# Delta rule: the triangular solve of both scan directions on four quadrants of the matmul array, with outputs, q k part, u and w in another order

## What is computed

```python
lower = jnp.where(strict, bc[..., :, None] * kk * decay, 0.0)
rhs = jnp.concatenate([vc * bc[..., None], kc * (bc * jnp.exp(gc))[..., None]], axis=-1)
sol = lax.linalg.triangular_solve(lower + jnp.eye(CHUNK), rhs, left_side=True, lower=True, unit_diagonal=True)
u, w = sol[..., :DV], sol[..., DV:]
qk = jnp.einsum("nbhid,nbhjd->nbhij", qc, kc) * decay

def step(S, xs):
    v_new = u_i - jnp.einsum("bhck,bhkv->bhcv", w_i, S)
    o = (jnp.einsum("bhck,bhkv->bhcv", q_i * jnp.exp(g_i)[..., None], S)
         + jnp.einsum("bhij,bhjv->bhiv", qk_i, v_new))
    S = S * jnp.exp(g_last)[..., None] + jnp.einsum("bhck,bhcv->bhkv", k_i * jnp.exp(g_last - g_i)[..., None], v_new)
```

## Time and profile before

| what | us |
|---|---|
| median of three runs | 2375.2 |
| lowest and highest of them | 2372.45 and 2375.28 |
| the profiled execution, its own time | 2375.22 |
| its span, first to last instruction | 2373.5 |
| setup of the DeltaNet phase to the first w, 404.70 to 435.72 | 31.02 |
| from the first to the eighth w, 435.72 to 740.77 | 305.05 |
| from there to the next phase, 740.77 to 775.50 | 34.73 |

### The profile page before, as it was taken

The page is one execution under the profiler, slowest core; times in us unless marked ns, Lnnn a source line. Parts: engine busy times, 40 slices in busy tenths (PEclk is TensorE's granted clock), DMA queues, the critical chain, the costliest instruction groups (busy, mean ns, idle before and its releaser), DMA issues. The chain is left out here.

```text
span 2373.5 us, 39379 instructions
## 1 busy us (share of the span) xinstructions
PE 2240.4 (94%) x15174; PEld 1811.4 (76%) x15174; DVE 1540.0 (65%) x1807; ACT 1193.4 (50%) x1387; POOL 419.5 (18%) x384
## 2 busy tenths in 40 slices
PE   5999999888988999999977999999999999999997
PEld 3777787777776777777866888888888888888885
DVE  5556311544544444464338988888989888898987
ACT  5232223233232333352216777777777676777675
POOL 6101201333231100000421101111111111111101
PEclk9999999999998999999978999999999999999998
DMA  8445542001001333166248999999999999999997
GB/s 295 160 142 159 162 122 66 3 20 38 20 20 33 100 101 107 63 219 194 107 169 306 356 385 393 385 384 384 383 382 380 383 394 385 382 384 381 382 383 283
DMA packets 271153, 557.51 MB, mean 235 GB/s; under 512 B 15672, under 2 KB 70045, under 8 KB 267965
## 3 DMA queue, kind: packets, MB, share of 16 engines
q1 hardware_dynamic: 261677, 530.16, 61.9%
q0 software_dynamic: 4752, 17.30, 2.7%
q10 hardware_dynamic: 4608, 8.39, 0.9%
HBM read 511.73 MB, written 44.07 MB: 234 GB/s over the span
## 5 line engine op out<-in xcount | busy, mean ns | idle before, releaser
L2605 PE MATMUL ps<-whigh,xeT 128*128 128x512 f32 x2048 | 657.1, 395 | 1.5 <-DVE xeT L2777 1.5
L2785 DVE TENSOR_TENSOR wlow<-hT,whigh 128x2048 fp32r<-128x2048 f32 x192 | 432.2, 2286 | 64.1 <-ACT whigh L2709 64.1
L2605 PEld LDWEIGHTS ps<-whigh,xeT 128*128 128x128 f32 x2048 | 385.8, 188 | 81.2 <-issue 1.9
L2605 PE MATMUL ps<-wlow,xeT 128*128 128x512 f32 x1024 | 399.6, 390 | 0.0
L2709 ACT ACTIVATE whigh<-hT 128x2048 fp32r<-128x2048 f32 x192 | 358.4, 1909 | 10.8 <-PE ps L2605 10.8
L2605 PE MATMUL ps<-whigh,hidT 128*128 128x512 f32 x1024 | 328.0, 391 | 0.0
L2785 DVE TENSOR_TENSOR wlow<-oaT,whigh 128x2048 fp32r<-128x2048 f32 x96 | 216.9, 2288 | 41.7 <-ACT whigh L2709 41.7
L2785 DVE TENSOR_TENSOR wlow<-obT,whigh 128x2048 fp32r<-128x2048 f32 x96 | 218.0, 2286 | 21.2 <-ACT whigh L2709 21.2
L2605 PEld LDWEIGHTS ps<-whigh,hidT 128*128 128x128 f32 x1024 | 192.3, 188 | 40.3
L2605 PEld LDWEIGHTS ps<-wlow,xeT 128*128 128x128 f32 x1024 | 193.2, 189 | 38.0
L2605 PE MATMUL ps<-wlow,hidT 128*128 128x512 f32 x512 | 199.6, 390 | 0.0
(11 more groups left out here) (329 smaller groups left out, 3554.2 us busy)
## 6 DMA issues: line engine op xcount, KB each, us to landing
hT<-in_w_down SPq DMA_DIRECT2D x66, 1024.0 KB, 10.4
obT<-in_w_up SPq DMA_DIRECT2D x64, 1024.0 KB, 10.6
hT<-in_w_up SPq DMA_DIRECT2D x64, 1024.0 KB, 8.4
hT<-in_w_gate SPq DMA_DIRECT2D x62, 1024.0 KB, 11.0
oaT<-in_w_down SPq DMA_DIRECT2D x62, 1024.0 KB, 8.8
oaT<-in_w_gate SPq DMA_DIRECT2D x34, 1024.0 KB, 10.4
obT<-in_w_gate SPq DMA_DIRECT2D x32, 1024.0 KB, 8.4
oaT<-in_w_ada SPq DMA_DIRECT2D x20, 1024.0 KB, 7.8
```

Of the source, the lines that this page charges most:

```text
L2605: mm = pe.matmul(out, lhs[x], rhs[y], start=start and i == 0, stop=stop and i == 2)
L2785: dve.tensor_tensor(wlow[slot][:, :], raw[(FIRST + x) % RAW_SLOTS], whigh[slot][:, :].bitcast(F32), ALU.subtract).then_inc(low_done, 1)
```

## The change

Level by level, both directions are now one group. y, inv_turn (the turn of the inverse, now also in level 0) and upd of levels 0 to 3 walk through four quadrants: the block in partition half h comes out in the half of its token pair, with the two source halves in two PSUM banks. POOL makes inv0 in one orientation. xb and inv hold both directions, and the transposes of x and of the q k part (xT, qkT) are separate tiles. Level 4 stays on two quadrants. The semaphores y_ps, y_sb, upd_ps, inv_done, invT_ps, invT_sb, w_ps and w_sb are no longer per direction.

The second gram product, make_qk and the turn of the q k part (qk_turn) move into levels 0 and 1 of the unit's own solve; rows of the next unit moves from level 0 to level 1, differences on DVE from levels 0 and 1 to 2 and 3. outputs is split: out_states after upd of level 3, out_chunks before upd of level 4. u is made ahead of w, and w and scan_kv are cut into four 64x64 quadrant matmuls. out_turn and tok_q stand before scan_ws of step 1; channels 1 and tok_v after scan_kv of step 1.

The functions on PE and its loop over units:

```diff
+def qk_turn(n):
+    pe.wait_ge(qk_done, n + 1)
+    pe.wait_ge(vb_done, 2 * n + 2)
+    for d in range(2):
+        mm = small_turns(2, d * HW, dec[:, d, :, :])
+    mm.then_inc(qkT_ps, 1)
+
+def to_slots(banks, left, right):
+
+    for t2 in range(TPG // 2):
+        for d in range(2):
+            for t in (2 * t2, 2 * t2 + 1):
+                for h in ((0, 1), (1, 0))[t % 2]:
+                    src = HALVES[h]
+                    lo = d * P + t2 * CHUNK
+                    mm = pe.matmul(ps[HALVES[t % 2], banks[h], lo:lo + CHUNK], left[src, d, t, :],
+                                   identc[src, :] if right is None else right[src, d, t, :], start=True, stop=True)
+    return mm
+
+def y(n, lv):
+    if lv == 0:
+        pe.wait_ge(xturn_sb, n + 1)
+        pe.wait_ge(qeT_sb, 2 * n + 2)
+        pe.wait_ge(inv0_done, 2 * n + 2)
     else:
+        pe.wait_ge(inv_done, n * LV + lv)
+    if lv < LV - 1:
+        mm = to_slots((0, 1), xT, inv)
...
+    mm.then_inc(y_ps, 1)
+
+def inv_turn(n, lv):
...
+    if lv < LV - 1:
+        mm = to_slots((4, 5), inv, None)
...
+def upd(n, lv):
+    pe.wait_ge(y_sb, n * LV + lv + 1)
+    pe.wait_ge(invT_sb, n * LV + lv + 1)
+    if lv < LV - 1:
+        for t2 in range(TPG // 2):
+            for d in range(2):
+                for h in range(2):
+                    for tp in ((0, 1), (1, 0))[h]:
+                        src = HALVES[tp]
+                        slot = 2 * t2 + h
+                        lo = d * P + t2 * CHUNK
+                        mm = pe.matmul(ps[HALVES[h], tp, lo:lo + CHUNK], invT[src, d, slot, :], xb[src, d, slot, :],
+                                       start=True, stop=True)
...
+def make_w(n):
+    pe.wait_ge(kbe_done, 2 * n + 2)
+    for d in range(2):
+        for t in range(TPG):
+            for turn_over in range(2):
+                for i, half in enumerate(HALVES):
+                    part = HALVES[(i + turn_over) % 2]
+                    lo = d * HW + t * CHUNK
+                    mm = pe.matmul(ps[part, 4 + i, lo:lo + CHUNK], kbe[d][half, t, part],
+                                   invT[half, d, t, :], start=True, stop=True)
+    mm.then_inc(w_ps, 1)
...
+    if i < NC1:
+        for turn_over in range(2):
+            for d in range(2):
+                t, half = place(chunks(d)[i])
+                part = HALVES[(d + turn_over) % 2]
+                mm = pe.matmul(ps[part, 6 + d, P:2 * P], kd[d][half, t, part], vnew[d][half, t, :],
+                               start=True, stop=True)
...
+def out_states(n):
+    if n + 2 < NU:
+        pe.wait_ge(diff_done, 2 * TPG * (n + 3))
...
+def out_chunks(n):
+    pe.wait_ge(vnew_done[0], (n + 1) * NC1)
+    pe.wait_ge(vnew_done[1], (n + 1) * NC1)
...
     for lv in range(LV):
+        y(n, lv)
+        inv_turn(n, lv)
+        if n >= 1 and lv == LV - 1:
+            out_chunks(n - 1)
         if n >= 1 and SPLIT + lv < NCHUNK:
             scan_ws(n - 1, SPLIT + lv)
+        if lv == 0:
+            gram(n, 1)
+        upd(n, lv)
+        if n >= 1 and SPLIT + lv < NC1:
             scan_kv(n - 1, SPLIT + lv)
+        if lv == 1:
+            qk_turn(n)
+            if more:
+                rows(n + 1)
+        if lv == 3:
+            if n >= 1:
+                out_states(n - 1)
+            if more:
+                tok_k(n + 1)
-    uw(n)
+    make_u(n)
+    make_w(n)
     scan_kv(n, 0)
     if more:
         channels(n + 1, 0)
+    if n >= 1:
+        out_turn(n - 1)
+    if more:
+        tok_q(n + 1)
     for i in range(1, SPLIT):
         scan_ws(n, i)
         if more:
             if i == 1:
                 gram(n + 1, 0)
             if i == 3:
+                x_turn(n + 1)
+        scan_kv(n, i)
+        if more:
+            if i == 1:
+                channels(n + 1, 1)
                 tok_v(n + 1)
+            if i == 3:
+                qe_turn(n + 1, 0)
+                qe_turn(n + 1, 1)
```

On ACT and DVE:

```diff
+def inverse_turned(n, lv):
+    act.wait_ge(invT_ps, n * LV + lv + 1)
...
+    if lv < LV - 1:
+        for d in range(2):
+            ins = act.activation(slots(invT, d, 0), crossed(4, 5, d), ACT.Copy)
+        ins.then_inc(invT_sb, 1)
...
+def mask_y(n, lv):
+    dve.wait_ge(y_ps, n * LV + lv + 1)
...
+    if lv < LV - 1:
+        for d in range(2):
+            ins = dve.tensor_tensor(slots(xb, d, 0), crossed(0, 1, d),
+                                    bcast(bcast(levelmask[:, d, lv + 1, :], 1, 2), 1, 2), ALU.mult)
+        ins.then_inc(y_sb, 1)
...
+def inverse(n, lv):
+    dve.wait_ge(upd_ps, n * LV + lv + 1)
+    if lv < LV - 1:
+        for d in range(2):
+            ins = dve.tensor_tensor(slots(inv, d, 1), slots(inv, d, 1), crossed(0, 1, d), ALU.subtract)
+        ins.then_inc(inv_done, 1)
```

More of the change, by code:

```diff
@@ L1221, in y @@
[L1221 to L1248, removed]
+                        pe.wait_ge(x_done[1], n + 1)
@@ new lines, in out_states @@
+                def out_states(n):
+                    if n + 2 < NU:
+                        pe.wait_ge(diff_done, 2 * TPG * (n + 3))
+                    else:
+                        pe.wait_ge(qk_done, NU)
+                    if n >= 1:
+                        pe.wait_ge(on_done, n)
+                    begun = set()
+                    for t in range(TPG):
+                        for d in range(2):
+                            for c in (2 * t, 2 * t + 1):
+                                if chunks(d)[0] != c:
+                                    half = place(c)[1]
+                                    pe.matmul(ps[half, 3, t * P:(t + 1) * P], qeT[n % 2][d][:, t, half], state[d][:, chunks(d).index(c), :],
+                                              start=c % 2 not in begun, stop=False, skip_group_check=True)
+                                    begun.add(c % 2)
@@ new lines, in out_chunks @@
+                def out_chunks(n):
+                    pe.wait_ge(vnew_done[0], (n + 1) * NC1)
+                    pe.wait_ge(vnew_done[1], (n + 1) * NC1)
+                    for t in range(TPG):
+                        for d in range(2):
+                            for half in HALVES:
+                                mm = pe.matmul(ps[half, 3, t * P:(t + 1) * P], qkT[n % 2][half, d, t, :], vnew[d][half, t, :],
+                                               start=False, stop=d == 1, skip_group_check=True)
+                    mm.then_inc(o_ps, 1)
@@ L1537, in _ @@
                 differences(0, 1)
-                for d in range(2):
-                    make_x(0, d)
-                    make_qk(0, d)
+                make_x(0, 0)
+                make_x(0, 1)
                 for n in range(NU):
@@ L1544, in _ @@
                         i = SPLIT + lv
[L1545 to L1551 removed]
+                        mask_y(n, lv)
@@ L1559, in _ @@
+                        inverse(n, lv)
                         if n >= 1 and i < NC1:
                             scan_state(n - 1, i)
[L1561 to L1564 removed]
+                        if lv == 0:
+                            make_qk(n)
+                        if lv == 2 and more:
+                            differences(n + 1, 0)
@@ L1583, in _ @@
+                        if i < 3 and more:
+                            make_x(n + 1, i - 1)
                 for i in range(SPLIT, NCHUNK):
```

352 lines of the change are left out of this document (155 added, 197 removed).

## The result

| | before | after |
|---|---|---|
| median of four runs | 2375.24 us (2372.45 to 2377.86) | 2340.61 us (2339.39 to 2344.19) |
| profiled execution, span | 2375.22, 2373.5 us | 2339.39, 2337.7 us |
| eighth unit's w (before) or u (after) less the first's | 305.05 us | 271.87 us |

The next phase begins at 739.65 us instead of 775.55, 35.9 earlier, and takes from there as long as before (1598.05 and 1597.95 us): all of it is in the changed phase.

The account below looks back on a forecast made before the run. PE was taken to set the pace in the DeltaNet phase: 2375.2 - 27 (shorter units) + 13 (clock falls before y) + 7 (falls in level 3) = 2368 to 2369, given as 2369.0; range 2348 to 2397, the forecast's own 2360 to 2376.

Parts of the forecast that it names:

- 277.3 + 20: First to last unit: 7 x 40.35 - 5.2 = 277.3 us at full clock, plus 13 and 7 for clock falls.
- Four quadrants: Solve, levels 0 to 3: sixteen matmuls cost what eight did, 0.47 us; a plain level falls from 3.88 to 3.6.
- Rival (c): Quadrants sharing rows or columns follow each other; y, turn, upd cost 0.47 more each, 45 us: 2412; 0.14 with milder form.
- The clock: TensorE falls to 1.2 GHz in idle stretches: seven falls cost 13 us, two units' falls in level 3 cost 7.
- a fall in every unit: Between scan_ws 1 and y: one clock fall per unit, 1.3 to 2.5 us, taken as 1.9; seven cost 13.
- falls in level 3: Idle time from upd of level 2 to out_states brings falls of 3.7 us in two units of seven: +7.
- The steps from u to y: After the solve, through the scan to the next unit's y: 16.45 us at full clock against 18.15.
- The solve: Levels 0 to 4, from y of level 0 to the next u: 23.9 us against 25.5.
- Setup: Before the first unit: comes out even, one orientation of inv0 less but y starts later.
- tail: After the last unit: loses about 0.5 us, since scan_kv waits for the pair and out_states gains it back.
- rival (a): No clock falls anywhere: 2375.2 - 27 = 2348 us; chance 0.14.

Follow-up runs that it names:

- the run on two quadrants: The changed kernel with y, turn and upd of levels 0 to 3 on two quadrants, as in level 4, order of work kept: 2371.85 us.
- the runs with extra matmuls: The changed kernel with seventeen extra matmuls per unit between gram and y: 2336.04 us; the same with out_states also moved to level 4: 2341.93 us.
- the run on order: The changed kernel with y, turn and upd doing the eight matmuls with equal halves first, then the eight that cross: 2357.03 us.
- the fastest kernel: The changed kernel with both qe_turn behind scan_kv 2, differences one level earlier, second make_x directly behind the first, x_turn behind scan_ws 2: 2323.36 us.

## Why the prediction was wrong, point by point

It gave 2369.0 and a range from 2348; 2340.6 lies below. From the first to the last unit it had 277.3 + 20 = 297.3 us against 271.87. By its own steps:

1. **Four quadrants** (sixteen matmuls in 0.47, plain level 3.6): right, 0.49 and 3.66 (646.61 to 650.27). Rival (c) is refuted; its price, 45 us, was too high: 31 in the run on two quadrants, where a plain level costs 1.1 more and not 1.4 (4.76 against 3.66); that other work hides a part and that one operation of 512 elements replaces two are the likely reasons, which no run separates. Sixteen matmuls have 32 passes, 0.49 us / 32 = 15 ns a start. On this the Trainium skill (TensorE: Matmul & The Clock Gate, section "Wait - 56ns, not 53.3ns?") has starts no closer than about 25 ns; by that rule the time would have been 2398, an estimate from the page's figure; the measured 15 ns, a mean over one group, decides against it for matmuls on four quadrants.
2. **The clock** (+20: seven falls at 1.9, two at 3.7 in level 3) is the step that failed most. There were four falls, all between u and y, at 16.70, 16.77, 16.64 and 16.58 against 15.57 us: 4.4 us in all, 15.6 less than I set. The place and the cause were right (the runs with extra matmuls), the price of 1.9 lies between the 1.0 to 1.5 measured in the traces for falls of 3.4 us and the 2.0 to 2.5 for falls of 6.8. What failed was "a fall in every unit": equal units at 511.22 and 590.89 went either way, as the earlier trace rows had already shown, and over all runs with that stretch 17 of 30 had a fall. I read the rows as a reason for a fall everywhere when they only said that it can happen. And no row supported falls in level 3; none came.
3. **The steps from u to y**: 16.45 predicted, 15.57 measured; with the first unit -6.0 over seven. It is the same small excess at several points: scan_kv 0 at 2.75 (2.9), scan_ws 1 at 5.41 (5.8), x_turn at 12.18 (13.1).
4. **The solve**: 23.9 predicted, 23.0 measured, -5.9 over seven. Level 3 was 5.62 (6.0), with the wait for dec that was foreseen but shorter; levels 1 and 2 together 8.17 (8.45); level 4 5.55 (5.8). DVE's pair of subtractions takes 0.75, not two times 0.42, and rows and the next y overlap on the array.
5. **Not foreseen**: pauses inside a group, some 2.0 us over the seven (six full solves sum to 140.0 us, 6 x 23.0 = 138.0).
6. Setup -0.7 and tail -2.6 against the prediction (32.72 us from the last u to the next phase, 34.78 before, where I had +0.5). What shortened the tail was not tested.

So -15.6 - 6.0 - 5.9 + 2.0 = -25.5 in the walk, and 3.3 outside it, make up the 29 us. Even rival (a), with no falls at all, stayed 7 us above the result, since a dozen handoffs were each rounded up.

## What to carry to other kernels

Where small matmuls set the pace, spread consecutive ones over all four quadrants: here that alone was worth 31 of 35 us, and a mere change of order among the same passes gave half of it back. A possible clock fall is a chance per stretch, to be priced at what falls cost in the rows times the share of like stretches that had one; extra matmuls in the waits removed it in the stretch where they stood. After such a step look again for who releases the next unit first: three moves without any new arithmetic gave 17 us more.

## What the runs showed of the hardware that was not expected

TensorE can start a pass for a free quadrant ahead of passes that stand before it in the program (621.28 and 621.32 in the run on order; level 1 of the changed kernel, where y starts inside rows):

```profile
653.99 0.82 PE L1165 MATMUL ps<-gsum,ones 64*64 64x256 f32 x6
654.44 0.34 PE L1228 MATMUL ps<-inv,xTd 64*64 64x64 f32 x4
654.64 0.38 PE L1165 MATMUL ps<-gsum,ones 64*64 64x256 f32 x2
```

And TensorE pauses in the middle of a group, with no releaser in the profile. The changed kernel, PE in order of time:

```profile
576.15 0.69 PE L1228 MATMUL ps<-identc,inv 64*64 64x64 f32 x30 [0.79 <-issue]
...
580.81 0.45 PE L1228 MATMUL ps<-identc,inv 64*64 64x64 f32 x11 [0.53 <-issue]
```

Between the first and the last u and at full clock, take the cases in which two matmuls of one group that follow each other start more than 0.3 us apart (a group being matmuls of one line on the same operands, waits for other engines left out). The traces of the kernel before, of two quadrants and of the changed order have none; the changed kernel has four, with the extra matmuls five, the fastest kernel seven, and the other runs one to six. Most stand in the turn of the inverse or in upd of levels 0 to 3, on four quadrants.

The traces hold a hint at the cause. In the changed kernel the only DMA packets from 575 to 592 us are three of the queue q8, of kind instruction (packets, MB, share of the DMA engines' time):

```profile
q8 instruction: 3, 0.05, 1.1%
```

It brings a packet of 16 KB every few us, and all 32 such pauses in the traces of the eight runs that have any end 1.2 to 1.6 us after the end of one of its packets: 1.27 and 1.24 us for the two shown, after the packets that start at 573.94 and 578.64. That TensorE's instructions arrive too late there is the reading that fits, but no run tested it, and most packets bring no pause. Why it is often the unit that starts near 550 us stays open, as does what decides between two equal stretches whether the clock falls.
